# Eight chunks of an expert pair: five of them in reloaded blocks of SBUF instead of a one-time early load, and the decay's sums taken with broadcast gates

## What is computed

```
gc = jnp.cumsum(to_chunks(g), axis=-1)
decay = jnp.where(tri, jnp.exp(jnp.where(tri, gc[..., :, None] - gc[..., None, :], 0.0)), 0.0)
m = jnp.einsum('bhncd,bhnsd->bhncs', k_beta, k) * decay
t_inv = lax.linalg.triangular_solve(m, eye, left_side=True, lower=True, unit_diagonal=True)
```

```
def expert_block(args):
    xb, e = args
    return (jax.nn.silu(xb @ w_eg[e]) * (xb @ w_eu[e])) @ w_ed[e]
...
y = yb.reshape(total_blk * MOE_BLOCK, dm)[dest] * gate_s[:, None].astype(h.dtype)
return jax.ops.segment_sum(y, tok_s, num_segments=n_tok).reshape(b, s, dm)
```

## Time and profile before

| | |
|---|---|
| median of 3 runs | 1903.46 us (1903.42 to 1903.55) |
| the profiled execution | 1900.37 us |
| its span in the trace | 1898.4 us |
| mean granted clock of PE | 0.996 |
| PE busy | 1813.2 us (96%) |
| DVE, ACT, POOL busy | 972.1, 685.5, 21.3 us |
| read from HBM | 480.77 MB, 254 GB/s over the span |

### The profile page before, as it was taken

How to read it: one execution, slowest core, us unless ns; L and a number is a source line. 1 busy time by engine, 2 the same in 40 slices (tenths; PEclk the granted TensorE clock), 3 DMA queues, 4 the chain that set the end, 5 groups by cost and what they waited for, 6 DMA issues and landing times.

```text
span 1898.4 us, 33058 instructions
## 1 busy us (share of the span) xinstructions
PE 1813.2 (96%) x13803; PEld 1482.2 (78%) x13803; DVE 972.1 (51%) x1401; ACT 685.5 (36%) x1052; POOL 21.3 (1%) x14
## 2 busy tenths in 40 slices
PE   8999989999999998999999899999999999999998
PEld 5999979999899986789998799888884444443433
DVE  3988668886874545454445896377531111111111
ACT  3444444444544425444444633456411110110101
POOL 0000000000000000000000111000000000000000
PEclk9999999999999999999999999999999999999999
DMA  9999619997475421245441332442456999999997
GB/s 389 424 375 339 232 68 356 344 339 265 182 307 189 177 90 67 107 194 179 186 176 59 131 134 101 160 174 101 165 201 281 414 425 426 425 424 425 425 425 304
DMA packets 46046, 483.45 MB, mean 255 GB/s; under 512 B 5105, under 2 KB 5233, under 8 KB 7153
## 3 DMA queue, kind: packets, MB, share of 16 engines
q1 hardware_dynamic: 45792, 480.79, 64.2%
q10 hardware_dynamic: 144, 1.05, 0.2%
HBM read 480.77 MB, written 1.05 MB: 254 GB/s over the span
## 4 chain that ended last, share of the span: by engine, by line
PE 42%; DMA 9%; DVE 3%; ACT 2%; issue 1%; DVEq 0%; SPq 0%; ACTq 0%
PE psG L415 26%; DMA ring<-stream 9%; PE psA L415 9%; PE psS L415 6%; DVE mem L2458 1%; PE psS L1361 0%; DVE parts L2144 0%; DVE mem L2716 0%; DVE mem L2228 0%; ACT mem L1571 0%; DVE st L2722 0%; PE psA L1013 0%; DVE mem L2456 0%; PE psS L1333 0%; DVE X L2237 0%
## 5 line engine op out<-in xcount | busy, mean ns | idle before, releaser
L415 PE MATMUL psG<-parts 128*128 128x256 f32 x6016 | 763.9, 285 | 13.8 <-DVE parts L2144 5.7
L415 PEld LDWEIGHTS psG<-parts 128*128 128x128 f32 x6016 | 736.7, 192 | 35.7 <-issue 19.2
L415 PE MATMUL psA<-parts 128*128 128x256 f32 x2368 | 303.2, 284 | 1.6 <-DVE parts L2317 1.6
L415 PEld LDWEIGHTS psA<-parts 128*128 128x128 f32 x2368 | 290.7, 192 | 17.7 <-issue 15.2
L415 PE MATMUL psS<-ring,mem 128*64 128x512 f32 (+1 forms) x1028 | 231.0, 595 | 21.4 <-DMA ring<-stream 18.5
L2082 DVE TENSOR_TENSOR parts<-ring,parts 128x2048 fp32r<-128x2048 f32 x80 | 183.1, 2289 | 116.9 <-ACT parts L1536 116.8
L415 PEld LDWEIGHTS psS<-ring,mem 128*64 128x64 f32 (+1 forms) x1028 | 72.2, 137 | 175.8 <-issue 129.4
L1536 ACT ACTIVATE parts<-ring 128x2048 fp32r<-128x2048 f32 x80 | 153.1, 1914 | 88.9 <-PE psA L415 88.4
L2073 DVE SCALAR_TENSOR_TENSOR mem<-ring,silc,mem 128x1536 f32<-128x1536 f32 (+1 forms) x98 | 138.9, 1417 | 2.5
L2312 DVE TENSOR_TENSOR mem<-mem,psS 128x512 f32<-128x512 f32 x16 | 11.0, 688 | 234.3 <-ACT mem L1990 234.3
L2144 DVE TENSOR_TENSOR parts<-ring,parts 128x1024 fp32r<-128x1024 f32 x76 | 92.9, 1230 | 59.5 <-ACT parts L1560 58.1
(11 more groups left out here) (356 smaller groups left out, 1568.2 us busy)
## 6 DMA issues: line engine op xcount, KB each, us to landing
ring<-stream SPq DMA_DIRECT2D x300, 1536.0 KB, 8.9
mem<-stream SPq DMA_DIRECT2D x9, 512.0 KB, 7.8
X<-x_in SPq DMA_DIRECT2D x1, 1024.0 KB, 17.6
ring<-stream SPq DMA_DIRECT2D x1, 1024.0 KB, 21.9
mem<-masks ACTq DMA_DIRECT2D x1, 1024.0 KB, 4.7
x_out<-X SPq DMA_DIRECT2D x4, 256.0 KB, 2.9
ring<-stream SPq DMA_DIRECT2D x1, 512.0 KB, 23.4
cst<-consts SPq DMA_DIRECT2D x1, 304.0 KB, 3.0
```

The source lines that it names most:

```text
L415: return nc.tensor.matmul(out, lhsT, rhs, start=start, stop=stop, skip_group_check=True)
```

## The change

SP loads eleven chunks ahead. `LATE = 5` of every pair's eight chunks no longer go through the ring but into five fixed triples of neighbouring blocks of `mem` (`LATE_AT = (4, 7, 10, 13, 23)`), one transfer of 12 KB rows each, with a semaphore `late_0` to `late_4` for each triple. Every pair reloads them. The first three chunks of a pair are in the ring, which so holds two pairs' worth. Every chunk now counts `chunk_used`, and the n-th load of the experts waits for the use of the (n - 11)-th chunk. SP's queue has them in this order, for pair p: as chunks 0, 1, 2 of pair p - 1 are used, chunks 0, 1, 2 of pair p + 1; then, as chunks 3 to 7 of pair p - 1 are used, chunks 3 to 7 of pair p. The first five late chunks wait for the mixer's last product (`hyb_acc`) and not for the norm's sums. The small tiles of the experts' stage move to other blocks (`SEL` from 4 to 0, `ROUTE` from 24 to 20, and so on). In the delta rule the two DVE products of `tri` and the product with the strict triangle are gone, and the two matmuls of `rows` become eight of 128 columns, with a gate's column, read 128 times over, as the stationary operand and the triangle as the moving one. `dense` is rewritten for the same blocks.

```diff
-            sp.wait_ge(sem("pre_sum"), 8)
-            for i, b in enumerate(EARLY_AT):
-                sp.dma_start(blk(b), stream[NCHUNK + i // 3, :, (i % 3) * SLOT:(i % 3 + 1) * SLOT])\
-                    .then_inc(sem("early_in"), 16)
...
+            c, n_ring = BASE["moe"], 8 - LATE
+            def pair(r, p, final=False):
+                free = c + 8 * (p - 1) + 1
+                for j in range(8):
+                    if j >= n_ring or not final:
+                        sp.wait_ge(chunk_used, r * 48 + (free + j))
+                    if j >= n_ring:
+                        late(r, p, j - n_ring)
+                    elif not final:
+                        in_ring(r, c + n_ring * (p + 1) + j)
...
+            sp.wait_ge(sem("hyb_acc"), 1)
+            for i in range(LATE):
+                late(0, 0, i)
+            sp.wait_ge(chunk_used, c)
+            in_ring(0, c + RING - 1)
+            pair(0, 1)
+            with sp.Fori(0, 2) as r:
+                for p in range(2, 8):
+                    pair(r, p)
+            pair(0, 14)
+            pair(0, 15, final=True)
...
-                after("gdn_dve", GD, "tri")
-                for b in range(2):
-                    last = mm(psA[:, b, :], ones, DEC[:, 4 * b:4 * b + 4, :].rearrange("p u s -> p (u s)"),
-                              start=True, stop=True)
+                for u in range(NU):
+                    h, n = divmod(u, 2)
+                    last = mm(psA[:, u // 4, (u % 4) * P:(u % 4 + 1) * P], unit_col(GG, h, n).to_broadcast([P, P]),
+                              MK[:, M_TRI:M_TRI + P], start=(u % 4 == 0), stop=True)
                 g_step("rows", last)
...
-            def half_used(r, p, g, ins):
-                if p or not isinstance(r, int) or g < 48 - 6 * EARLY:
-                    ins.then_inc(chunk_used, 1)
+            def half_used(ins):
+                ins.then_inc(chunk_used, 1)
...
-                tri = MK[:, M_TRI:M_TRI + P][:, None, :].to_broadcast([P, GH, P])
-                V.tensor_tensor(DEC[:, 0:NU:2, :], tri, per_unit(GG, 0), ALU.mult)
-                g_step("tri", V.tensor_tensor(DEC[:, 1:NU:2, :], tri, per_unit(GG, 1), ALU.mult))
...
-                link(V.tensor_tensor(DECL[:, 1:NU:2, :], DEC[:, 1:NU:2, :], per_unit(BETA, 1), ALU.mult))
-                strict = MK[:, M_STRICT:M_STRICT + P][:, None, :].to_broadcast([P, NU, P])
-                g_step("decl", V.tensor_tensor(DECL, DECL, strict, ALU.mult))
+                g_step("decl", V.tensor_tensor(DECL[:, 1:NU:2, :], DEC[:, 1:NU:2, :], per_unit(BETA, 1), ALU.mult))
```

More of the change, by code:

```diff
@@ L26 @@
 RING = 6
-EARLY = 3
+LATE = 5
 EPS = 1e-6
@@ new lines, in late, with in_ring @@
+            def late(r, p, i):
+                n = NCHUNK + LATE * p + i
+                src = stream[n, :, :] if isinstance(r, int) else \
+                    stream[bass.ds(r * (6 * LATE) + n, 1), :, :].rearrange("o p n -> (o p) n")
+                sp.dma_start(blk(LATE_AT[i], 3), src).then_inc(sem(f"late_{i}"), 16)
+            def in_ring(r, n):
+                src = stream[n, :, :] if isinstance(r, int) else \
+                    stream[bass.ds(r * (6 * n_ring) + n, 1), :, :].rearrange("o p n -> (o p) n")
+                sp.dma_start(ring[:, n % RING, :], src).then_inc(full[n % RING], 16)
@@ L396, in build @@
         POS = blk(22)[:, 64:128].rearrange("p (t e) -> p t e", t=TT)
[L398 to L401, removed]
+        SEL = blk(0)[:, 0:512].rearrange("p (b t s) -> p b t s", b=2, t=TT)
+        GSL = blk(0)[:, 512:514]
+        SELT = part(1)[:, 0:512].rearrange("p (b s) -> p b s", b=2)
+        YS = part(2, 2).rearrange("p (h n) -> p h n", h=2)
         HTOK, XE = tiles(16, 2, D), tiles(18, 1, P)
-        LGX, EX, FO = blk(24)[:, 704:704 + S], blk(24)[:, 256:266], blk(24)[:, 192:228]
+        ROUTE = blk(20)
+        LGX, EX, FO = ROUTE[:, 704:704 + S], ROUTE[:, 256:266], ROUTE[:, 192:228]
         HT = blk(19)[:, 0:512].rearrange("p (f s) -> p f s", f=FE)
         HACT, HSIL = blk(21)[:, 0:512], blk(21)[:, 512:1024]
-        GB = blk(4, 8)
-        HD = tiles(12, 2)
+        GB = blk(0, 4), blk(16, 4)
+        HD = tiles(21, 2)
         @block.tensor
@@ L1306, in pair_half, with half_arrived @@
             def pair_half(r, p, g, a=0, n=512):
[L1308 to L1319, removed]
[L1320 to L1325 removed]
+                if g < 48 - 6 * LATE:
+                    return half(BASE["moe"] + (8 - LATE) * p, g, a, n)
+                a += (g % 6) * 512
+                return blk(LATE_AT[(g - 48 + 6 * LATE) // 6], 3)[:, a:a + n]
+            def half_arrived(r, p, g):
+                if g < 48 - 6 * LATE:
+                    arrived(pe, BASE["moe"] + (8 - LATE) * p + g // 6, r * (6 * (8 - LATE)))
+                else:
+                    pe.wait_ge(sem(f"late_{g // 6 - 8 + LATE}"), r * (6 * 16) + 16 * (p + 1))
+            def half_used(ins):
+                ins.then_inc(chunk_used, 1)
             def sparse():
@@ L1353, in gate_up @@
                                 if g % 6 == 5:
-                                    half_used(r, p, g, last)
+                                    half_used(last)
                     last.then_inc(sem("sp_gu"), 1)
@@ L1378, in down @@
                                 if g % 6 == 5:
-                                    half_used(r, p, g, last)
-                        if h == 0 or (p == 0 and isinstance(r, int)):
+                                    half_used(last)
+                        if h == 0:
                             last.then_inc(sem("sp_dn"), 1)
@@ L1464, in step @@
                                 if g % 6 == 5:
-                                    half_used(r, p, g, last)
+                                    half_used(last)
                 step(0, 0)
-                with pe.Fori(0, 5) as r:
-                    for j in range(3):
-                        step(r, 1 + j)
-                pe.wait_ge(chunk_used, NCHUNK)
+                step(0, 1)
+                with pe.Fori(0, 2) as r:
+                    for j in range(6):
+                        step(r, 2 + j)
+                for p in range(14, NP):
+                    step(0, p)
+                pe.wait_ge(chunk_used, BASE["moe"] + 8 * NP)
                 pe.sem_inc(sem("moe_acc"), 4)
@@ L2952, in _pack_stream @@
     import numpy as np
-    out = np.zeros((NCHUNK + EARLY, P, CHUNK), np.float32)
+    out = np.zeros((NCHUNK + NP * LATE, P, CHUNK), np.float32)
     def put(name, parts, at=0):
@@ L3060, in _pack_stream @@
                 o[:, g // 6, :, g % 6] = down[e::2, f, :, h]
-    o, c, n = o.reshape(NP * 8, P, CHUNK), BASE["moe"], 8 - EARLY
-    out[c:c + n], out[c + n:NCHUNK], out[NCHUNK:] = o[0:n], o[8:], o[n:8]
+    o = o.reshape(NP, 8, P, CHUNK)
+    out[BASE["moe"]:NCHUNK] = o[:, :8 - LATE].reshape(-1, P, CHUNK)
+    out[NCHUNK:] = o[:, 8 - LATE:].reshape(-1, P, CHUNK)
     return out
```

60 lines of the change are left out of this document (30 added, 30 removed).

## The result

| | before | after |
|---|---|---|
| median of 5 runs each, us | 1903.42 (1901.65 to 1903.55) | 1894.47 (1890.84 to 1897.14) |
| ratio, 95% interval | | 0.995 (0.9935 to 0.9965) |
| profiled execution, us | 1900.37 | 1894.47 |
| its span, us | 1898.4 | 1892.5 |
| its mean granted clock | 0.996 | 0.994 |

The changed kernel is 9.0 us faster by the medians; 10.2 were forecast. The profiled execution of after is only 5.9 faster than that of before. That gap is part of what has to be explained, since it isn't where the look-ahead works. The interval of the ratio stands for a gain of 6.7 to 12.4 us, so the medians alone can't tell 9.0 from 7.6 or from 10.2; the traces can.

A forecast was written before the change was run, and what follows sets the result against it. The prediction took transfers (29.72 us a pair) to bound the experts from pair 4 and DVE the decay; 7.6 us from look-ahead plus 2.6 from decay made 10.2, from 1903.46 to 1893.3 us, range 1890.0 to 1897.0.

The forecast's parts named there:

- The bound and the count: Experts: transfers bound later pairs; last wait is chunk 5 of pair 14, 105 loads into the run; 7.6 us less.
- the 8.8 us said to be left lying: Experts' load order: of 16.4 us of stock, 8.8 stays in the ring because three loads too early go first.
- This costs nothing: Experts' late chunks of pair 0 go out as the mixer's last product ends, not at 1406.77; no cost.
- The decay's 2.58 us: Mixer's decay: removing DVE's products, 1.33 and 1.25 us, moves all that follows up to the experts by 2.58 us.
- The weight loads: Eight `rows` products on PE: 2.02 us with 16 loads beside them; by the skill's rule, an estimated 1.7 us more.
- The whole stock pays: Rival, experts: PE's last wait is for the end of all loads, 16.4 us less, 1884.5 with the decay; chance 0.07.
- The transfers get slower: Rival, experts' loads: at 2% slower 1901.1 us, no change; at 5% 1912.8; chance 0.11.
- Decay gives nothing: Rival, mixer's decay: ACT or PE is just behind DVE, so only the 7.6 us remain, 1895.9; chance 0.10.
- the forecast's own bounds: Decay 0 to 2.6 us and look-ahead 5.5 to 9.7, giving 1891.2 to 1898.0 us at the ends.

The follow-up runs named there:

- late_after_norm: The changed kernel with the first five late chunks waiting for the last norm's sums, as before the change; 1895.38 us.
- decay_alone: The kernel before with only the decay's part of the change added; 1901.01 us, ratio 0.9993.
- order_from8: The changed kernel with each pair's five late chunks issued ahead of the next pair's three ring chunks from pair 8 on; 1885.16 us, run again 1885.04.
- ahead_alone: The changed kernel with the decay's part undone, so the look-ahead alone; 1894.29 us, ratio 0.9956.
- from8_without_decay: The changed kernel with late chunks ahead of the next pair's ring chunks from pair 8 on, and the decay's part undone; 1887.95 us, ratio 0.9913.

## Why the prediction was right, point by point

**The bound and the count.** The count of loads up to the last wait is the part that carried the prediction, and it held to 0.3 us: resume in pair 14, first wait in pair 7, none in pair 15, and 29.73 us a pair in between ((1843.82 - 1695.18) / 5, from resume to resume; 29.7 forecast). The runs on order and depth tested it from both sides. With the three ring loads behind the late chunks, the 8.8 us said to be left lying came out as 8.8 on the traces and as 9.3 by the medians (1894.47 to 1885.16); with one chunk less of stock the time rose by 5.4 by the medians.

**"This costs nothing"**, of the earlier first load: confirmed, by `late_after_norm`: 455.45 us behind pair 0's start against 455.37.

**The decay's 2.58 us.** This term was too large in two ways. At fill 12 it is 2.13. The missing 0.45 is in DVE's low part of fill 10, which runs beside POOL's second product:

```profile
1072.31 2.40 POOL L2936 TENSOR_TENSOR mem<-mem 128x1024 f32<-128x1024 f32 x1 [0.41 <-ACT mem L1852]
1073.70 2.09 DVE L2162 TENSOR_TENSOR parts<-ring,parts 128x1024 fp32r<-128x1024 f32 x1
```

Before, the same pair of instructions:

```profile
1074.53 2.38 POOL L2922 TENSOR_TENSOR mem<-mem 128x1024 f32<-128x1024 f32 x1
...
1076.35 1.64 DVE L2144 TENSOR_TENSOR parts<-ring,parts 128x1024 fp32r<-128x1024 f32 x1
```

The low part alone takes 1.23. It runs into POOL's product by 0.56 before and by 1.01 after, and is 0.41 and 0.86 longer. POOL's product begins behind ACT's result and came only 2.22 earlier, DVE 2.65, and DVE gave the difference back. The sentence that failed is "I take the whole 2.58 us, as all that follows up to the experts moves by it": it asked of PE and ACT, not of POOL. So nearly the whole overlap is lost, not a share of it. The Trainium skill ("SBUF — State Buffer", Who interferes with whom) says that a DVE instruction with two inputs in SBUF contends with a GpSimd one that reads SBUF, and that such contention is an exclusive lock. The trace agrees to 0.15 us, both times.

The second way is the falls of the clock: none behind fill 12 in before's profiled execution, two in after's. They make 3.0 us, more than the decay gave, and one kernel without the decay's part has them too. By the medians the decay's part is worth 2.0 (`decay_alone`, 1902.98 against 1901.01, not told from none), nothing (1894.29 without it, 1894.47 and 1894.24 with it), and 2.8 us (on `order_from8`; 2.0 and 2.3 against before in the same series); at equal clock 0.8 to 2.1, which goes with the 2.13 that the trace shows at its place. The step that fails here is the plain sum: a term of 2.6 us stood beside a scatter of up to 9 us between the runs of one kernel, of which the forecast said nothing. The three runs of before that it had lie within 0.13 us. On the traces the parts make 7.7 + 2.1 = 9.8 us, less what the falls take; that the medians of five runs give 9.0 is in part luck.

**The weight loads.** The eight products with gates broadcast over 128 columns take 1.95 us with 16 loads in 1.87 beside them, where 2.02 was forecast. The rule of the Trainium skill ("TensorE: Matmul & The Clock Gate", part 3) that a load overlaps only with a matmul of another row group would have cost an estimated 1.7 us here; this trace disagrees as that of before did.

**The rivals.** "The whole stock pays" is refuted for this order of loads and is what `order_from8` does: 1884.5 was named, 1885.1 measured. "The transfers get slower": 424 GB/s, no. "Decay gives nothing", 1895.9, can't be excluded by the times: it lies within the stated range, and 1894.47 is about halfway between it and 1893.3. The traces show 2.13 us of gain at its place. The upper end of the range, 1897.0, is also 1 us below the 1898.0 of the forecast's own bounds; nothing hung on it.

**Not foreseen:** PE is 2.03 us late in pair 8, at the return of its loop, where the old kernel had it under a wait. Between two waits for transfers it cost nothing there. `order_from8` has 1.91 us of it at 1647.91.

## What to carry to other kernels

When transfers bound a loop and PE starts from stock, don't look at the loop's rate but count: how many loads must have landed at the last wait, and when does the unbroken run begin? Each load that is queued ahead of the one waited for makes it a transfer's time later: here three ring loads, 3 x 3.715 = 11.1 us at chunk 5 of pair 14. Of these 8.8 reach the end, for an order that changes no byte; the rest comes back since pair 15 has no ring loads in front and goes at PE's pace instead of the transfers'. The best version is the changed kernel with that order from pair 8 on, 1885.1 us, 18 below before and 9 below the change.

When a few microseconds are taken out of one engine's chain, look at every engine that works beside it at that place, and compare one part of a trace by the time from a landmark to a landmark before you believe the ends.

## What the runs showed of the hardware

- DVE's product of 1024 columns took 1.23 us alone and 1.64 or 2.09 when it began under POOL's product. The other way round, POOL's first product, begun 0.11 us behind DVE's, took 3.37 in place of 2.40.
- TensorE's clock fell to 1.2 GHz (granted clock 0.50) in the mixer of the changed kernel's profile, once behind 3.72 us of products with 8 rows, once behind a stretch with waits (from 1314 to 1316 PE was busy for 0.92 us). Each of these falls cost 1.5 us. Of the twelve profiles, before and `ahead_alone` have no such fall between fill 12 and pair 0 and the others two or more, `from8_without_decay` the second at 1237 and not near 1316; the runs of one kernel lie up to some 9 us apart (before: 1900.25 to 1909.7 over all series), more than the decay's whole term. What decides it was not found.
